# Two fused transformer blocks on one Trainium2 core: the residual kept in the experts' PSUM sums, two more expert halves in flight, norms by token rows, ScalarE's order in the up product, and splits inside the gate rows

## What is computed

```
first block:  h = rmsnorm(x); x = x + hybrid_mixer(h)        # mLSTM heads + pooling, products with w_in and w_out
              h = rmsnorm(x); x = x + moe_ffn(h)             # 32 experts, top 4, SwiGLU, d_ff 1024
              x = rmsnorm(x, normf_g)
second block: hn = rmsnorm_2(x); forgetting attention and gated delta rule, w_in_2 is 1024 x 9240
              x = x + (gated sum of the two branches) @ w_out_2
              hn = rmsnorm_2(x); up = causal_dwconv(hn @ w_up_2)      # 1024 x 5632, three taps
              x = x + (silu(gate) * value) @ w_down_2                 # 2816 x 1024
              return rmsnorm_2(x, norm_final_2)
```

## Time and profile before

| | |
|---|---|
| median of 3 runs | 1740.4 us (1739.36 to 1742.21) |
| the profiled execution | 1741.8 us, its span 1740.1 us |
| mean granted TensorE clock | 0.988 of full |
| PE busy, DVE, ACT, POOL | 97%, 35%, 25%, 17% of the span |
| HBM read | 505 MB |

### The profile page before, as it was taken

One profiled execution on the slowest core, in us unless ns is written; L12 is line 12 of the kernel. 1 busy time (PEld: TensorE's weight loads), 2 busy tenths in 40 slices (PEclk: granted clock), 3 DMA queues, 4 the chain that ended last, 5 costly groups with the idle time before them and its releaser, 6 DMA issues. The chain is left out here.

```text
span 1740.1 us, 23039 instructions
## 1 busy us (share of the span) xinstructions
PE 1689.1 (97%) x9318; PEld 973.8 (56%) x9318; DVE 614.2 (35%) x1136; ACT 439.0 (25%) x640; POOL 290.0 (17%) x185
## 2 busy tenths in 40 slices
PE   9998999999999999999999999999999999999998
PEld 7654333333333333333333333888898899989986
DVE  4233212122121212211112122773575443468762
ACT  2111111110111111111111111763355353443433
POOL 1200000000000000000000000536144423434552
PEclk9997999999999999999999999999999999999999
DMA  9443999999999999999999999342143115545452
GB/s 351 177 159 137 427 426 428 428 428 428 428 428 428 428 428 428 428 428 428 428 428 428 428 428 371 101 146 97 50 146 140 55 49 181 177 139 184 156 193 97
DMA packets 92612, 507.38 MB, mean 292 GB/s; under 512 B 8955, under 2 KB 32552, under 8 KB 67976
## 3 DMA queue, kind: packets, MB, share of 16 engines
q1 hardware_dynamic: 92408, 506.00, 71.9%
q10 hardware_dynamic: 144, 0.52, 0.1%
HBM read 505.46 MB, written 1.05 MB: 291 GB/s over the span
## 5 line engine op out<-in xcount | busy, mean ns | idle before, releaser
L1298 PE MATMUL ps<-ring,xg 128*64 128x512 f32 x1536 | 339.9, 596 | 8.4 <-DMA ring<-in_w_up 8.4
L184 POOL TENSOR_TENSOR low<-ring,high 128x1024 fp32r<-128x1024 f32 x81 | 203.9, 2522 | 285.8 <-ACT high L181 283.2
L1298 PEld LDWEIGHTS ps<-ring,xg 128*64 128x64 f32 x1536 | 107.5, 137 | 238.0 <-issue 217.6
L1409 PE MATMUL ps<-hTh,high 128*128 128x256 f32 x800 | 230.4, 288 | 9.4 <-DVE low L184 8.3
L1410 PE MATMUL ps<-hTl,high 128*128 128x256 f32 x800 | 227.7, 285 | 0.0
L1411 PE MATMUL ps<-hTh,low 128*128 128x256 f32 x800 | 227.6, 284 | 0.0
L181 ACT CAST high<-ring 128x1024 fp32r<-128x1024 f32 x162 | 165.8, 1046 | 156.1 <-PE ps L1411 82.0
L1330 PE MATMUL ps<-ring,aT 128*64 128x512 f32 x768 | 175.4, 598 | 0.0
L184 DVE TENSOR_TENSOR low<-ring,high 128x1024 fp32r<-128x1024 f32 x81 | 109.7, 1354 | 164.0 <-ACT high L181 163.8
L1720 POOL MEMSET X<- 128x1024 f32 x1 | 1.0, 952 | 996.9 <-POOLq L1103 996.9
L1409 PEld LDWEIGHTS ps<-hTh,high 128*128 128x128 f32 x800 | 154.7, 193 | 14.0 <-issue 14.0
(11 more groups left out here) (418 smaller groups left out, 2293.3 us busy)
## 6 DMA issues: line engine op xcount, KB each, us to landing
ring<-in_w_down SPq DMA_DIRECT2D x53, 2048.0 KB, 27.4
ring<-in_w_gate SPq DMA_DIRECT2D x48, 2048.0 KB, 25.4
ring<-in_w_up SPq DMA_DIRECT2D x48, 2048.0 KB, 26.9
ring<-in_w_in SPq DMA_DIRECT2D x23, 2048.0 KB, 8.2
extra<-in_w_gate SPq DMA_DIRECT2D x16, 2048.0 KB, 24.8
extra<-in_w_up SPq DMA_DIRECT2D x16, 2048.0 KB, 27.5
extra<-in_w_down SPq DMA_DIRECT2D x16, 2048.0 KB, 31.6
ring<-in_w_up SPq DMA_DIRECT2D x22, 1024.0 KB, 6.7
```

The costliest lines, as they stand in the source:

```text
L184: eng.tensor_tensor(lo, self.raw(u), hi.bitcast(F32), ALU.subtract).then_inc(self.sem(who + "_split"), 1)
L1298: last = pe.matmul(bank[h * CAP:(h + 1) * CAP, :], xg[:, c, kh, :], w[:, c, h * 512:(h + 1) * 512], start=False, stop=kh == 1 and c == 3)
L1409: pe.matmul(out, wh, xh, start=start, stop=False)
```

## The change

It has seven parts.

1. Experts' sums: banks 4 to 7 are started by the product identity x x instead of zeros, so that they hold x plus all experts. At the end DVE multiplies each bank with the final gain into x, and ACT squares the banks themselves in phase B. Phase C loses the product with the gain; the residual becomes x * r1. The expert loop's small buffers lie in x's storage.
2. Pieces: a new tile `spare` holds pieces 8 and 9, which are loaded in phase A (9 after the pooling product, 8 after the output product); mixer buffers share its storage. Piece n from 10 on goes into place (n - 2) % 8. The first four experts are written out, the loop starts with round 1. The first two pieces of phase C are loaded after the gate halves of the last expert.
3. Norms by token rows in phase A ("n2"), in phase E ("nn") and at the end ("fin"): squares of halves, and one root, reciprocal and scale for each row; each row is transposed by itself. The fillers of phase A become three, between the rows, and those in front of the rank products go.
4. Gate rows: one more unit is rounded by ACT (`ahead(8)`), and DVE makes the low part of unit 10 inside the gate rows.
5. The last splits of phase C end one unit earlier (`UNITS_E + 11`).
6. Phase E: the second half of the output product runs one token row after the other (`rows_in_turn`), with later units split between the rows' norms.
7. Phase D: ACT does the Silu of pass j behind the rounding of the product of pass j - 1 and of two more units. The last four units of the down product go first for row 0, then for row 1; the last norm and the stores are made by rows and halves.

```diff
+        spare = sb("spare", [P, 2, PIECE], stack=ab)
...
+    def row_norm(self, v, chain, tag, n, t, eps):
+
+        c = self.stat[:, 4 * n + t:4 * n + t + 1]
+        r = self.stat[:, 4 * n + 2 + t:4 * n + 3 + t]
+        v.wait_ge(self.sem("norm_squares"), self.squares_by(tag)[t])
+        chain(v.tensor_tensor(c, c, r, ALU.add))
+        v.tensor_scalar(c, c, 1.0 / D, eps, ALU.mult, ALU.add).then_inc(self.sem("norm_mean"), 1)
+        v.wait_ge(self.sem("norm_root"), self.nth(tag) + t)
         chain(v.reciprocal(r, c))
-        for t in range(NT):
...
+    def row_transposes(self, pe, banks, tag, t):
+
+        if t == 0:
+            for j in range(KC // 2):
+                banks.claim(pe, (tag, j))
+        pe.wait_ge(self.sem("norm_scaled"), NT * (self.scaled(tag) - 1) + t + 1)
+        for j in range(KC // 2):
+            bank = banks.ps[:, banks.at[tag, j][0], :]
+            for c in (2 * j, 2 * j + 1):
+                o = (c % 2) * S + t * P
+                last = pe.transpose(bank[:, o:o + P], self.xn[:, t, c * P:(c + 1) * P], self.ident[:, :])
+            if t == NT - 1:
+                banks.filled(last, (tag, j))
...
+    def at(self, n, first):
+
+        return n if first and n < self.SLOTS else (n - self.SPARE) % self.SLOTS
+
...
-            for n, use in ((0, ("qk", 3)), (1, ("v", 1)), (2, ("u", 1)), (3, ("o", 1)), (6, ("ym", 1)), (7, ("ym", 1)),
-                           (4, ("out", 0, 1)), (5, ("out", 1, 1))):
+            for n, use in ((0, ("qk", 3)), (1, ("v", 1)), (2, ("u", 1)), (3, ("o", 1)), (9, ("pool", 1)),
+                           (6, ("ym", 1)), (7, ("ym", 1)), (4, ("out", 0, 1)), (5, ("out", 1, 1)), (8, ("out", 1, 1))):
                 banks.done(sp, use)
-                pieces.load(sp, A, n, n // 6)
+                pieces.load(sp, A, n, n // 6, True)
...
-            def summed(t):
+            for t in range(NT):
                 for n in range(2):
                     banks.moved(act, ("out", n, t))
-
-            k.squares(act, "n2", 1, hT[:, :, :].rearrange("p (t c) n -> p t (c n)", t=NT), summed)
-            k.root(act, "n2", 1)
+                    k.squares_of(act, t, n, 1, hT[:, :, :].rearrange("p (t c) n -> p t (c n)", t=NT))
+                k.row_root(act, "n2", 1, t)
             banks.done(act, "gates")
...
-            k.scale(v, chain, "n2", 1, EPS1, by_row_of_four)
+                k.row_scale(v, chain, "n2", 1, t, EPS1, by_row_of_four)
...
-            keep_busy(pe, banks.claim(pe, ("n2", 0)), ones, 7)
-            k.transposes(pe, banks, "n2")
+            k.row_transposes(pe, banks, "n2", 0)
+            keep_busy(pe, banks.claim(pe, "lg"), ones, 3)
+            k.row_transposes(pe, banks, "n2", 1)
...
-                pe.matmul(banks.ps[:, b, :], zero_row[:, 0:P], zero_row[:, :], start=True, stop=False)
+                pe.matmul(banks.ps[:, b, :], ident[:, :], x[:, (b - 4) // 2, (b % 2) * 512:(b % 2 + 1) * 512],
+                          start=True, stop=False)
             bank = banks.claim(pe, "rk")
-            keep_busy(pe, bank, ones, 3)
...
+            for n in range(Pieces.SLOTS + Pieces.SPARE, 32):
+                used = n - Pieces.SLOTS - (Pieces.SPARE if n < 2 * Pieces.SLOTS + Pieces.SPARE else 0)
+                freed(used, used // Pieces.PER)
+                pieces.load(sp, A, n, n // Pieces.PER, True)
+            with sp.Fori(1, last) as rnd:
...
-            before_last = sp.snap(Pieces.ROUND * last + Pieces.ROUND - 1)
-            sp.wait_ge(sem("first_half_used2"), before_last)
+            steps = sp.snap(Pieces.ROUND * last + Pieces.ROUND)
+            sp.wait_ge(sem("first_half_used0"), steps)
             load_c(sp, A, env["ringC"], 0)
-            bank_done(sp, DOWN, before_last)
+            bank_done(sp, GATE, steps)
             load_c(sp, A, env["ringC"], 1)
 
         @block.vector
...
-                    xs = x[:, t, h * 512:(h + 1) * 512]
-                    v.tensor_tensor(xs, xs, total(t, h), ALU.add).then_inc(sem("residual_summed"), 1)
+                    c = slice(h * 512, (h + 1) * 512)
+                    v.tensor_tensor(x[:, t, c], total(t, h), env["gain"][:, c], ALU.mult).then_inc(sem("gained"), 1)
...
+                act.wait_ge(sem("gained"), 2 * t + 2)
+                act.activation(xn[:, t, :], banks.ps[:, SUM + 2 * t:SUM + 2 * t + 2, :].rearrange("p h n -> p (h n)"),
+                               ACT.Square, accum_out=stat[:, 8 + t:9 + t]).then_inc(sem("norm_squares"), 1)
...
+            for r in range(Pieces.ROUND):
+                expert(r, r, None)
+            with pe.Fori(1, pe.snap(passes_of(pe) * (NE // Pieces.ROUND))) as rnd:
                 for r in range(Pieces.ROUND):
...
+def rows_in_turn(pe, units, banks, u, keys, xh, xl):
+
+
+    for t in range(NT):
+        bank = banks.claim(pe, keys[t])
+        a = slice(t * P, (t + 1) * P)
+        for kc in range(KC):
+            q, c = kc // 2, kc % 2
+            if t == c == 0:
+                units.ready(pe, u + q)
+            wh = units.buf(units.high, u + q)[:, c * 512:(c + 1) * 512]
+            wl = units.buf(units.low, u + q)[:, c * 512:(c + 1) * 512]
+            pe.matmul(bank, xh[:, kc, a], wh, start=kc == 0, stop=False)
+            pe.matmul(bank, xh[:, kc, a], wl, start=False, stop=False)
+            last = pe.matmul(bank, xl[:, kc, a], wh, start=False, stop=kc == KC - 1)
+            if t and c:
+                units.finish(last, u + q)
+        if t == 0:
+            banks.filled(last, keys[0])
...
-            k.squares(act, "nf", 2, flat)
             for t in range(NT):
-
-                act.wait_ge(sem("norm_scaled"), NT * (k.nth("nf") - 1) + t + 1)
-                act.activation(work[:, t].rearrange("p t n -> p (t n)"), xn[:, t, :], ACT.Square, accum_out=stat[:, 12 + t:13 + t])\
+                act.activation(work[:, t].rearrange("p t n -> p (t n)"), x[:, t, :], ACT.Square, accum_out=stat[:, 12 + t:13 + t])\
                     .then_inc(sem("norm_squares"), 1)
                 if t == 0:
...
-                ahead(7)
+                ahead(8)
...
-            ahead(UNITS_E + 12)
+            ahead(UNITS_E + 11)
...
-                v.tensor_tensor(xn[:, t, :], x[:, t, :], gain[:, :], ALU.mult).then_inc(sem("norm_scaled"), 1)
...
-                v.scalar_tensor_tensor(x[:, t, :], x[:, t, :], r1[:, t:t + 1], gain[:, :], ALU.mult, ALU.mult)\
-                    .then_inc(sem("residual"), 1)
+                v.tensor_scalar(x[:, t, :], x[:, t, :], r1[:, t:t + 1], None, ALU.mult).then_inc(sem("residual"), 1)
...
+                units.ahead(v, "low0", 8)
...
+                    if n:
+                        k.row_root(act, "nn", 0, t)
+                        units.ahead(act, "high", UNITS_OUT + 7 + t)
...
+                    if n:
+                        k.row_scale(v, chain, "nn", 0, t, EPS2)
+                        ahead(UNITS_OUT + 6 + 2 * t)
...
-            for n in range(2):
-                rows(pe, units, banks, UNITS_OUT + 4 * n, [("out", n, t) for t in range(NT)], mix_high, mix_low,
-                     lambda q: pe.wait_ge(sem("mix_low"), q + 1))
+            rows(pe, units, banks, UNITS_OUT, [("out", 0, t) for t in range(NT)], mix_high, mix_low,
+                 lambda q: pe.wait_ge(sem("mix_low"), q + 1))
+            rows_in_turn(pe, units, banks, UNITS_OUT + 4, [("out", 1, t) for t in range(NT)], mix_high, mix_low)
...
-            keep_busy(pe, banks.claim(pe, ("nn", 0)), ones, 8)
-            k.transposes(pe, banks, "nn")
+            k.row_transposes(pe, banks, "nn", 0)
+            keep_busy(pe, banks.claim(pe, ("up", 0, 0)), ones, 8)
+            k.row_transposes(pe, banks, "nn", 1)
...
-                banks.moved(act, ("up", j, 0))
-                act.activation(cv[:, j % 2, 0], cv[:, j % 2, 0], ACT.Silu).then_inc(sem("up_silu"), 1)
                 if j:
                     act.wait_ge(sem("up_act"), j)
                     act.copy(act_high[:, 2 * j - 2:2 * j, :], cv[:, (j - 1) % 2, 1]).then_inc(sem("act_high"), 1)
                 units.ahead(act, "high", U0 + 4 * j + 4)
+                banks.moved(act, ("up", j, 0))
+                act.activation(cv[:, j % 2, 0], cv[:, j % 2, 0], ACT.Silu).then_inc(sem("up_silu"), 1)
...
+                r = k.row_norm(v, chain, "fin", 1, t, EPS2)
+                v.wait_ge(sem("norm_final_in"), 16)
+                for n in range(2):
+                    c = slice(n * 512, (n + 1) * 512)
+                    v.scalar_tensor_tensor(res[:, t, c], x[:, t, c], r, gain[:, c], ALU.mult, ALU.mult)\
+                        .then_inc(sem("norm_scaled"), 1)
...
+            tail = range(FF_CHUNKS - Units.BUFS, FF_CHUNKS)
...
+                for t in range(1 if c in tail else NT):
                     for n in range(2):
-                        wh = units.buf(units.high, u)[:, n * 512:(n + 1) * 512]
-                        wl = units.buf(units.low, u)[:, n * 512:(n + 1) * 512]
```

(10 more changed lines are left out.)

168 lines of the change are left out of this document (96 added, 72 removed).

## The result

The changed kernel takes 1712.5 us in the median of 4 runs (1708.04 to 1714.74), against 1741.3 of the kernel before: a ratio of 0.984, with a 95% interval from 0.982 to 0.986. It is faster, as forecast, and inside the range of 1697 to 1716; the forecast was 1707. The profiled execution is the shortest of the four: 1708.0 us, its span 1706.0, its mean granted clock 0.996.

The account below looks back on a forecast made before the run. PE is busy 97% of the span, with DMA feeding late phase B and late splits or meetings stopping PE elsewhere. Eight terms sum to 33.2 us, from the profiled 1741.8 to 1708.6, or 1707 from the median; range 1697 to 1716.

Parts of the forecast that it names:

- Router stretch: Phase A's end to the experts: full-height bank products, norm by rows and no fillers save 8.2 us (bounds 4.3 and 9.5).
- Pieces: Phase B's weight loads: two more pieces give a lead of only 1.3 us (0.5 to 9.8), with DMA idle 8.5 us.
- Gate rows: Phase C: unit 10's low part made inside the gate rows removes PE's stop, saving 4.5 us (bounds 1.5 and 5.7).
- C to E: Meeting of phases C and E: last split a unit earlier saves 3.5 idle plus 2.2 clock, 5.7 us (3.0 to 6.0).
- norm: Norm of phase E: row 0 is done before, fillers then hold the rest up; saves 1.1 us (0.5 to 1.8).
- up and down product: Phase D: Silu last in ACT's pass breaks the circle of waits, PE never stops; saves 10.4 us.
- tail: Kernel's end: last scale is half a row's pair and last store a quarter; saves 1.5 us (0.8 to 2.0).
- the rival built on that rule: Up product: DVE stays the pace through POOL's units or late Silu; 8.7 of 10.4 us lost, 1716 us, chance 0.12.

Follow-up runs that it names:

- the two exchanges of height: Router stretch's four bank products: full height in place of one row on the kernel before, 1735.5 us; one row in place of full height on the changed kernel, 1713.7 us.
- full height alone: The kernel before with its four bank products made of the identity by x in place of the row of zeros: 1735.5 us, ratio 0.994.
- tall rows: The changed kernel with phase C's eight-row products, which spread decay and beta rows, given 128 rows with zeros below: 1702.8 us, ratio 0.977.
- unit 12 split early: The changed kernel with unit 12 rounded right behind the gate rows and its low part made ahead of two convolutions: 1714.2 us, ratio 0.983.

## Why the prediction was right, and where it was not

*Router stretch*: right in kind, 9.65 for 8.2. The full-height products keep the upper level, which the two exchanges of height show; with them alone 6.85 us of it come (output product to first weights 45.82 us before, 38.97 with full height alone), and the norm by rows with the fillers gone the other 2.8 (36.15). I had the four products right and the rest of the stretch too small: rank products, gather and what lies behind them gained 2.7 us and not 1.3 (7.0 + 0.4 + 0.9 is 8.3 and not 8.2, a slip in the sum). The 1.55 us ahead of it belong to no part of the change that I can name: in the profile before the same products ran at a mean clock of 0.57 from 46 to 50, behind products of four rows. It fell there in 5 of the 13 profiles of this case: in all four of the kernel before and its variants, and in one of the changed kernel, the one with tall rows. Whether the change makes it rarer is not shown.

*Pieces*: right. The hole came, 7 us long (8.5 forecast), the last copy moved 1.0 us beyond its start, and filling the places again gave most of the lead back, 5.2 us.

*Gate rows*: the step that failed. "PE need not stop: 3.7 + 1.4 = 5.1", less up to 2 for unit 12. The stop was back in full at unit 12, 3.17 us, with the lower clock behind it, and 1.3 us were left of 4.5 (4.83 less the 3.52 at the meeting). Behind it lies a second error, which the run with unit 12 split early showed: DVE's queue of convolutions is the next bound of this stretch, so a stop taken from PE alone comes back where PE needs the squares. The prediction had called what ACT's extra rounding delays on DVE covered, and had expected the shorter residual product to move DVE's queue up. The queue did not end earlier: DVE makes 1.2 us more inside the gate rows, and its last product there ends only with a unit of POOL (1.91 us for 0.28), so that its last convolution ends 51.0 us behind the first product of phase C, against 50.5 before, though its queue began 0.9 earlier.

*C to E, norm, up and down product, tail*: right. 3.52 and about 2.2 for 5.7; 1.6 for 1.1; 10.32 for 10.4; 1.8 for 1.5. Two single edits on the kernel before confirm two of them, 8.7 + 1.6 of the up and down product and 3.5 + 2.15 of the meeting of C and E. By the Trainium skill (SBUF — State Buffer, Who interferes with whom) a DVE instruction with two SBUF inputs and a GpSimd instruction that reads SBUF shut each other out for a whole instruction. The trace agrees, 1.34 us for a product that takes 0.69 alone and 1.91 for a low part of 1.22. But DVE met it only twice a pass, 1.3 us in all, and had room for that, so the rival built on that rule fell.

*From span to median*: the sum met the span, and the median of 1712.5 lies 5.5 us above the forecast. The unsaid step was that the profile's clock is a run's typical clock. It was for the kernel before (0.988, median 0.988); for the changed kernel the profiled execution is the best of ten (0.996, median 0.9935), 3.2 us by 1.27 us per 0.001. A second step was too good as well: 1.4 us were taken off because the profiled execution lay above the median of three runs, but over 44 runs the median is 1742.2, above the profiled 1741.8. Why a clock falls behind eight-row products in one execution and not in the next stays open.

## What to carry to other kernels

Read a stop together with every queue that ends behind it: the time is won only if the engine that feeds the next meeting is earlier too. A product of few rows costs more than its columns say, by the weight load that is no longer hidden when the height changes and by the clock that tends to fall behind it; zeros up to 128 rows cost no time that a run here shows. Compare runs at an equal granted clock where less than one per cent matters.

## What the runs showed of the hardware

- An eight-row product among products of 128 rows cost 0.39 us more than a tall one at an unchanged clock (a head with two of them 2.53 us against 1.75); among its like it cost nothing more (0.43 us between starts in both kernels).
- In all eleven profiles with the eight-row products, the clock fell to 0.50 for 3 to 13 us behind them at one or more of their places, with PE busy; in the two with tall rows at none of these places. By the Trainium skill (TensorE: Matmul & The Clock Gate, Part 1: The HAM clock gate) the clock follows how busy PE has been; these falls came while PE was busy all the time, so here the height of the products mattered beside it.
- Run time follows mean granted clock on one line, 1.27 us per 0.001, with a scatter of 0.6 to 0.8 us: nearly all of the spread of these kernels' runs is the clock.
